# A delta rule on one core: from one queue of steps per direction to one round per engine

## The reference, cut to what matters

```
def rwkv7_scan(r, w, k, v, kk, a, reverse):
    """S_t = S_{t-1} diag(w_t) + (S_{t-1} (-kk_t)) (kk_t * a_t)^T + v_t k_t^T,  y_t = S_t r_t."""
    def step(s, inp):
        r_t, w_t, k_t, v_t, kk_t, a_t = inp
        sa = jnp.einsum('bhvk,bhk->bhv', s, -kk_t)
        s = (s * w_t[:, :, None, :] + sa[..., None] * (kk_t * a_t)[:, :, None, :]
             + v_t[..., None] * k_t[:, :, None, :])
        return s, jnp.einsum('bhvk,bhk->bhv', s, r_t)
y = (rwkv7_scan(r, heads(w_f), k, v, kk, a, False)
     + rwkv7_scan(r, heads(w_b), k, v, kk, a, True))
```

## Time and profile before

| | us |
|---|---|
| median of three runs | 3620.04 (3617.94 to 3622.69) |
| the profiled execution, device time | 3625.01 |
| its span in the trace | 3623.7 |
| PE busy | 3422.7 (94%) |
| DVE busy | 2096.0 (58%) |
| ACT busy | 1322.2 (36%) |
| POOL busy | 65.4 (2%) |

### The profile page before, as it was taken

How to read it: one execution, slowest core, us unless ns; L and a number is a source line. 1 busy time by engine, 2 the same in 40 slices (tenths; PEclk the granted TensorE clock), 3 DMA queues, 4 the chain that set the end, 5 groups by cost and what they waited for, 6 DMA issues and landing times.

```text
span 3623.7 us, 56068 instructions
## 1 busy us (share of the span) xinstructions
PE 3422.7 (94%) x23384; PEld 2802.9 (77%) x23384; DVE 2096.0 (58%) x3889; ACT 1322.2 (36%) x2452; POOL 65.4 (2%) x32
## 2 busy tenths in 40 slices
PE   7989899999999889999999999999888989999999
PEld 6767688888888677788888887766666778778887
DVE  6776653643357667634544368653656579674434
ACT  4456543342224465443333233222322234232222
POOL 0000000000000000000000000000000034000000
PEclk9999999999999999999999989999999999999999
DMA  4221123333333212223333233234100323243332
GB/s 134 76 66 47 53 76 106 98 94 99 98 118 103 66 59 57 61 76 116 94 99 99 94 107 85 79 87 144 46 21 21 117 64 122 88 133 99 96 96 87
DMA packets 353827, 315.37 MB, mean 87 GB/s; under 512 B 11348, under 2 KB 281812, under 8 KB 353576
## 3 DMA queue, kind: packets, MB, share of 16 engines
q1 hardware_dynamic: 352712, 309.56, 27.8%
q10 hardware_dynamic: 864, 2.23, 0.2%
HBM read 288.15 MB, written 23.59 MB: 86 GB/s over the span
## 4 chain that ended last, share of the span: by engine, by line
PE 75%; DVE 16%; ACT 5%; issue 3%; DMA 1%; POOL 0%; SPq 0%; DVEq 0%; ACTq 0%; POOLq 0%
PE banks L528 12%; PE banks L530 12%; PE banks L529 12%; PE banks L427 8%; PE banks L429 8%; PE banks L428 8%; DVE weights_r L368 2%; PE banks L3098 2%; ACT weights_high_r L361 1%; PE banks L628 1%; PE banks L2622 1%; PE banks L1100 1%; PE banks L1113 1%; PE banks L2641 1%; ACT probabilities L1249 1%
## 5 line engine op out<-in xcount | busy, mean ns | idle before, releaser
L368 DVE TENSOR_TENSOR weights_r<-weights,weights_high_r 128x1024 fp32r<-128x1024 f32 (+3 forms) x520 | 605.2, 1172 | 382.1 <-ACT weights_high_r L361 381.1
L528 PE MATMUL banks<-h_T_hi,weights_high_r 128*128 128x512 f32 (+2 forms) x1904 | 759.7, 399 | 15.0 <-issue 3.9
L530 PE MATMUL banks<-h_T_hi,weights_r 128*128 128x512 f32 (+2 forms) x1904 | 737.6, 387 | 0.0
L529 PE MATMUL banks<-h_T_lo,weights_high_r 128*128 128x512 f32 (+2 forms) x1904 | 737.1, 387 | 0.0
L361 ACT ACTIVATE weights_high_r<-weights 128x1024 fp32r<-128x1024 f32 (+3 forms) x520 | 510.6, 992 | 360.8 <-DMA weights<-in_w_mlp 212.9
L528 PEld LDWEIGHTS banks<-h_T_hi,weights_high_r 128*128 128x128 f32 x1904 | 361.7, 190 | 104.6 <-issue 32.5
L530 PEld LDWEIGHTS banks<-h_T_hi,weights_r 128*128 128x128 f32 x1904 | 361.3, 190 | 72.7
L529 PEld LDWEIGHTS banks<-h_T_lo,weights_high_r 128*128 128x128 f32 x1904 | 361.9, 190 | 69.9 <-issue 3.9
L427 PE MATMUL banks<-weights_high_r,h_T_hi 128*128 128x512 f32 (+3 forms) x704 | 292.4, 415 | 10.3 <-ACT cellsX L577 6.0
L429 PE MATMUL banks<-weights_high_r,h_T_lo 128*128 128x512 f32 (+3 forms) x704 | 268.2, 381 | 0.0
L428 PE MATMUL banks<-weights_r,h_T_hi 128*128 128x512 f32 (+3 forms) x704 | 268.1, 381 | 0.0
(11 more groups left out here) (571 smaller groups left out, 5476.3 us busy)
## 6 DMA issues: line engine op xcount, KB each, us to landing
weights<-in_w_in SPq DMA_DIRECT2D x182, 512.0 KB, 3.7
weights<-in_w_mlp SPq DMA_DIRECT2D x128, 512.0 KB, 3.8
weights<-in_ffn_w_in SPq DMA_DIRECT2D x44, 512.0 KB, 3.7
weights<-in_w_out SPq DMA_DIRECT2D x24, 512.0 KB, 3.6
weights<-in_ffn_w_down SPq DMA_DIRECT2D x22, 512.0 KB, 3.2
weights<-in_w_mem_kv SPq DMA_DIRECT2D x16, 512.0 KB, 3.6
weights<-in_w_diff_o SPq DMA_DIRECT2D x16, 512.0 KB, 3.5
weights<-in_w_mla_o SPq DMA_DIRECT2D x8, 512.0 KB, 3.3
```

The source lines that it names most:

```text
L368: ve.e.tensor_tensor(self.part(c.w_raw_r, u), self.part(c.w_raw, u), self.part(c.w_high_r, u).bitcast(F32), ALU.subtract).then_inc(*ve.tel ...
L528: pe.e.matmul(out, lhsT=wh[:, k, :], rhs=hi[k][:, cols], start=(k == 0), stop=False)
L529: pe.e.matmul(out, lhsT=wh[:, k, :], rhs=lo[k][:, cols], start=False, stop=False)
L530: mm = pe.e.matmul(out, lhsT=wl[:, k, :], rhs=hi[k][:, cols], start=False, stop=(k == self.chunks - 1))
```

## The change

The seven generators of preparation and step are gone. `round_pe`, `round_act` and `round_dve` write one whole round for both directions: the step of chunk n and the preparation of chunk p = n+1. In each stretch both directions' `prod` come first, then the other products, then both `w step`, then both `t step`.

- The scalings of chunk p+1 are made during the levels of chunk p: the exponentials by ACT after level 3 (`scaled_act`), `a` by DVE in level 4 (`queries_dve`), `b` and the end decay by DVE in level 5 (`keys_dve`). `r` and `k` are made by GpSimd (`rest_pool`), which waits for the exponentials and for `rk` of chunk p.
- `x`, and then `low`, `w` and `low t` of the next chunk, stand in one stretch; `sa` comes in the next, `y` and `state` of direction 0 in level 1 and of direction 1 in level 2, between `prod` and `w step`. DVE's `y_dve` stands ahead of its `cut` and subtractions of that level.
- `low` is copied by ACT without its mask (the masks of the levels cut it). The first four chunks' `y` are copied by ACT, not by DVE. The state products of the last chunk are left out, and its two updates of `z`. The column of ones in `ep` is set once.
- `self.n` is 2 + 13 * 8 + 3 = 109 places over the same 41.37 blocks, all of which are used.

The core of the diff (long functions cut):

```diff
-        self.n = 1 + 13 * (self.CHUNKS + 1)
+        self.n = 2 + 13 * self.CHUNKS + 3
...
-        ve.e.tensor_tensor(o["a"], self.kk[:, :, tc], ep[:, :, before_at], ALU.mult).then_inc(*ve.step())
-        ve.wait_ge("decay_out", n, d)
-        ve.e.tensor_tensor(u["b"], self.b[:, :, tc], em, ALU.mult).then_inc(*ve.tell("scaled_key", n, d))
-        ve.e.tensor_tensor(u["k"], self.key[:, :, tc], em, ALU.mult).then_inc(*ve.step())
-        ve.e.tensor_tensor(o["r"], self.r[:, :, tc], ep[:, :, sums_at], ALU.mult).then_inc(*ve.step())
-        ve.e.tensor_copy(o["decay"], ep[:, :, end:end + 1]).then_inc(*ve.tell("scaled_all", n, d))
...
+    def rest_pool(self):
...
+                if p > 1:
+                    gp.wait_ge("filled", "y", p - 2, d)
+                gp.wait_ge("decay_in", p, d)
+                gp.e.tensor_tensor(o["r"], self.r[:, :, tc], u["ep"][:, :, sums_at], ALU.mult).then_inc(*gp.step())
+                if p:
+                    gp.wait_ge("filled", "rk", p - 1, d)
+                gp.wait_ge("decay_out", p, d)
+                gp.e.tensor_tensor(u["k"], self.key[:, :, tc], u["em"], ALU.mult).then_inc(*gp.tell("scaled_rest", p, d))
...
+        for lev in range(1, 6):
+            for d in both:
+                u, o = self.parts(p, d)
+                pe.wait_ge("cut", p, d, lev)
+                pe.wait_ge("w_level", p, d, lev - 1)
+                self.swapping(("prod", p, d, lev), u["cut"], o["w"])
+            if lev < 3 and now:
+                self.y_pe(n, lev - 1)
...
+            for d in both:
+                u, o = self.parts(p, d)
+                pe.wait_ge("emptied", "prod", p, d, lev)
+                pe.wait_ge("t_level", p, d, lev - 1)
+                self.swapping(("w step", p, d, lev), u["t"], u["prod"])
+            for d in both:
+                u, o = self.parts(p, d)
+                if lev < 5:
+                    self.multiply(("t step", p, d, lev), (u["prod"], u["t"]))
+            yield
...
+        for lev in range(1, 6):
+            if lev < 3 and now:
+                self.y_dve(n, lev - 1)
...
+            if lev < 5:
+                for d in both:
+                    self.cut_dve(p, d, lev + 1)
+            if lev == 4:
+                self.queries_dve(p + 1)
+            elif lev == 5:
+                self.keys_dve(p + 1)
+            yield
```

More of the change, by code:

```diff
@@ new lines, in round_act @@
+    def round_act(self, n):
+        c, ac, p, both = self.c, self.c.ac, n + 1, range(2)
+        now, ahead = n >= 0, n + 1 < self.CHUNKS
+        if now:
+            for d in both:
+                ac.wait_ge("filled", "x", n, d)
+                if n:
+                    ac.wait_ge("filled", "sa", n - 1, d)
+                ac.e.activation(self.halves(self.units[d]["x"]), self.shared("x", n, d), ACT.Copy).then_inc(*self.taken(ac, "x", n, d))
+        if ahead:
+            for d in both:
+                self.wait_written(ac, "low", p, d)
+                if p:
+                    ac.wait_ge("cut", p - 1, d, 5)
+                ac.e.activation(self.halves(self.units[d]["low"]), self.shared("low", p, d), ACT.Copy).then_inc(*self.taken(ac, "low", p, d))
+        yield
+        if now:
+            for d in both:
+                ac.wait_ge("filled", "sa", n, d)
+                if n:
+                    ac.wait_ge("filled", "y", n - 1, d)
+                ac.e.activation(self.units[d]["sa"], self.got("sa", n, d), ACT.Copy, scale=-1.0).then_inc(*ac.frees("sa", n, d))
+        if ahead:
+            for d in both:
+                for name in ("vtok", "btok"):
+                    self.token_act(name, p, d)
+        yield
+        if not ahead:
+            return
+        for d in both:
+            self.token_act("ktok", p, d)
+        yield
+        for lev in range(1, 6):
+            for d in both:
+                u = self.units[d]
+                ac.wait_ge("filled", "prod", p, d, lev)
+                if lev > 1:
+                    ac.wait_ge("filled", "t step", p, d, lev - 1)
+                elif p:
+                    ac.wait_ge("filled", "w step", p - 1, d, 5)
+                ac.e.activation(self.halves(u["prod"]), self.swapped("prod", p, d, lev), ACT.Copy).then_inc(*ac.frees("prod", p, d, lev))
+            if lev < 3 and now:
+                self.y_act(n, lev - 1)
+            yield
+            if lev == 3:
+                self.scaled_act(p + 1)
+            yield
@@ L2718, in prepare_act, with pe @@
+    def pe(self):
+        c = self.c
+        c.pe.wait_all(self.ready)
+        if c.turns["scans"] % 2:
+            c.next_of("scans")
         yield
         yield
[L2721 to L2738, removed]
@@ L2853, in pe @@
-    def pe(self):
-        self.c.pe.wait_all(self.ready)
-        yield
-        yield from rounds(self.prepare_pe(0, 0), self.prepare_pe(0, 1))
-        for n in range(self.CHUNKS):
-            ahead = [self.prepare_pe(n + 1, d) for d in range(2)] if n + 1 < self.CHUNKS else []
-            yield from rounds(self.step_pe(n, 0), self.step_pe(n, 1), *ahead)
-        self.c.pe.stamp("rwkv scan")
+        for n in range(-1, self.CHUNKS):
+            yield from self.round_pe(n)
+        c.pe.stamp("rwkv scan")
@@ L3713, in pool @@
     def pool(self):
+        self.rule.rest_pool()
         self.hgrn.scores_pool()
```

341 lines of the change are left out of this document (202 added, 139 removed).

## The result

The changed kernel took 3599.97 us (median of 4 runs, 3598.48 to 3603.15), the kernel before 3621.36 beside it: a ratio of 0.994, 95% interval 0.9927 to 0.9952. It is faster by 21 us, inside the range and on the forecast side, but a little less than half of the 45 us that I forecast.

The account below looks back on a forecast made before the run. The rule was taken as a chain of hand-overs with PE in the middle, no engine full. 42.7 + 4 + 1.0 - 1.2 - 1.5 = 45.0 us off 3625.0 gave 3580.0, forecast 3575 as the median ran 5 lower; range 3555 to 3604.

Parts of the forecast that it names:

- The waits for other engines: Seven full rounds: PE's waits and low clock fall from 10.6 to 4.5 us a round, 42.7 us in all.
- PE's own issue: Full rounds: PE's products of both directions take 20.0 us of a 38.5 us round, from distances between starts.
- The second rival: Rounds: DVE's longer stretches, queues of both directions and POOL meetings leave 7.5 us of waits a round; 3600; chance 0.22.
- GpSimd: `r` and `k` scalings: 0.5 us an operation (range to 1.9), not late; two meetings with DVE cost 0.9 us a round.
- The fourth rival: GpSimd operations of 2.9 us lengthen DVE's chain in levels 4 and 5: 12 us slower, 3632; chance 0.05.
- The low clock: Rounds: stretches of PE at the low clock still cost 1.0 us a round after the change.
- the first rival: Rounds: more falls away, waits of 2.5 us a round, low clock going with the quiet stretches; 3558; chance 0.17.
- The first chunk: Preparation of the first chunk, 32.3 us with about 9 of waits: gains 4 us.
- my terms for the end: Behind the rounds: two `state` products dropped gain 1.0 us; `DeltaNorm` closer behind the rule costs 1.5 (0 to 6).
- The third rival: End: `DeltaNorm` stalls the full 6 us, late weights cost another 5 to 10; 3588; inside the forecast's 0.52.
- Signs: Round near 33 us; PE's idle for `cut` and `b` gone, the rest ended by DVE's `w` subtraction; POOL operation 0.5 to 0.8.

Follow-up runs that it names:

- The runs with a half and a whole packet: Changed kernel with one first-chunk product made five or nine times ahead of the rounds (128 or 256 PE instructions more): 3590.56 and 3603.92 us.
- The lightened DVE: Changed kernel with DVE's cuts and masks writing one pair of heads of four from the third chunk on (not computing the rule): 3602.78 us, ratio 0.9951.
- the row of products: Changed kernel with one first-chunk `prod` of level 1 made 61 times in a row instead of once: 3615.87 us, one run.

## Why the forecast was twice the gain

Against the 45.0 us of my sum, which went by the profiled execution, the profiled spans gave 25.3. Of the 19.7 that are missing, 16.3 are stops, which my sum did not have.

- **The waits for other engines**, the main term. I had 10.6 us a round of waits and low clock in the kernel before, and 4.5 in the changed one. The list of waits shows idle time alone, 39.6 us against 11.1, 28.5 of the 42.7; the rest of that term should be clock and the part of a hand-over that isn't idle, which no run prices. Its size was about right: the rounds are 20.4 us shorter with two more blocks in them, 3.5 us at 1.74, and with the 16.3 us of added stops that makes 40.2 of the 42.7. Of the whole, the spans without the stops are 3619.0 (3623.7 - 4.7) and 3577.4, 41.6 us apart, where I summed 45.0. `cut` and `b` are gone from the list in the rounds.
- **The step that failed** is PE's own issue, "20.0 us a round", from distances between starts inside one product, 0.28 us. I took it as a pace that PE can hold, with nothing in the sum for the supply of instructions. The runs showed 21.0 us of stops in its place, 3.0 a round, against 0.7 before. A round has 2043 records of PE and PEld ((7151 + 7152) / 7), 8 packets; at 3.5 us each they need 28 us of a round, and where they stand without waits or blocks between them PE stops. In the kernel before its waits for data gave the packets their time, with 4.7 us of stops left. Taking those waits away let 16.3 us (21.0 - 4.7) come back as stops. The runs with a half and a whole packet show what stops cost: only four repetitions of one product are between them, and 10 us of stops, 13 us of the rule and 13 us of the median move together. That the stops came back because the waits went is read from the lists and from the kernel before, whose stops stay at 4.7 and 6.5 us at two places of the packets' ends.
- **The second rival** named the time, 3600, and 7.5 us of waits a round, but for DVE's queue and GpSimd. The lightened DVE and the scalings back on DVE show that these are not it. Its number was right by luck, its cause wrong.
- **GpSimd**: the operation takes 0.76 to 0.91 us, where I took 0.5 out of 0.5 to 1.9; its meetings with DVE cost DVE 0.86 us a round, where I had 0.9, and the rounds no time that the runs can tell. The rule of the Trainium skill's SBUF — State Buffer, section Who interferes with whom, which I had cited, agrees in direction: only operations with both inputs in SBUF are longer. The fourth rival (slower from 2.4 us an operation) is out.
- **The low clock**: six of seven rounds run at 1.00 and one at 0.95, where before five stood below 1.00. I had left 1.0 us a round for it; most of it went, as the first rival had it. The rule of the Trainium skill that I had set beside it (TensorE: Matmul & The Clock Gate, HAM oscillation) agrees in direction with these rows: PE's idle time in the rounds fell from 44.3 to 32.1 us by the lists, and the clock rose from 0.95 to 0.99. No run changes the clock by itself.
- **The first chunk**: 0.5 us and not 4. It holds five blocks now, four before, 1.7 us, and its window ran at 0.89 (0.95 before). At equal blocks some 2 of the 4 us were there. Ahead of the very first `low` PE waits 1.6 us for `b`, which stands behind both `a` now and is longer beside GpSimd, 0.94 us and not 0.42:

```profile
2554.45 0.70 DVE L2712 TENSOR_TENSOR cellsS<-cellsB,small 128x256 f32<-128x256 f32 x1
2554.83 0.90 POOL L2746 TENSOR_TENSOR cellsE<-cellsA,cellsE 128x256 f32<-128x256 f32 x1
2555.08 0.94 DVE L2724 TENSOR_TENSOR cellsE<-cellsE 128x256 f32<-128x256 f32 x1
...
2556.07 0.70 PE L2622 MATMUL banks<-cellsE,cellsM 64*64 64x64 f32 x16 [1.57 <-DVE cellsE L2724]
```

  The two longer operations, 0.28 and 0.52 us more than 0.42, are half of that wait: here GpSimd did cost time on the chain.
- **The end**: 4.4 us come from behind the rounds; the three blocks that moved into rounds and first chunk are worth 4.2 (1.4 each), so my terms for the end (+1.0, -1.5) came to about 0. The third rival did not come.
- **Signs**: I said that what is left would be ended by the `w` subtraction (L2968). It is there with 0.3 to 0.5 us a time, but the longest rows are `issue`.

## What to carry to other kernels

When waits are taken out of an engine that issues many short instructions, divide its instructions by the time that is left: a page row of the instruction queue (packets and MB) and one unbroken row of products give the pace that it can hold. Idle rows ended by `issue` in the middle of a group of equal instructions are the sign of it. Where the rate is near that pace, a few instructions more or less ahead of a loop can be worth as much as a change inside it, so two variants must be compared at several such places before one is called better. By that rule the change of this study stands: with the packets' ends at five places ahead of the rounds it took 3590.6 to 3603.9 us, the kernel before at two places 3620.4 and 3621.4.

## What was not expected of the hardware

- PE's instructions came in packets of 256, one in 3.47 to 3.74 us in the row of products, where PE uses them up in 2.09 us (3.2 us was the shortest distance between two packets in any trace here). The idle time at each is 1.4 to 1.65 us in that row.
- A change between transposes and fp32 products on PE cost about 0.17 us each time (an estimate from the rows of `vtok`).
- The time of this kernel moved by 13 us (3590.6 to 3603.9) with 64 to 256 repeated PE instructions ahead of 250 us of rounds.
